# First feed-forward: the 512 columns of the gate and up products streamed in other orders

## The chip, the cores and the metric

The kernel runs on one core of a Trainium2 chip. The metric is the time in device microseconds of one execution. Two runs of the kernel before took 3107.92 and 3108.51 us, median 3108.22.

## The reference

Two transformer blocks for 256 tokens of width 2048, all in float32. The part that the change touches is the first feed-forward of the first block, with 5632 inner columns:

```python
def _swiglu(h, w_gu, w_down):
    gate, up = jnp.split(h @ w_gu, 2, axis=-1)
    return (jax.nn.silu(gate) * up) @ w_down

x = x + ... _swiglu(_rmsnorm(x, ffn1_norm), ffn1_w_gu, ffn1_w_down)   # first feed-forward
# then token mixing, a second feed-forward of the same size, and a second block of two layers
```

`h @ w_gu` is a product of 256 x 2048 by 2048 x 11264. It is summed over the 2048 rows of `w_gu`, column by column, so no column of the result depends on any other column.

## The kernel before

**Slabs.** All large weights come from memory as a stream of slabs of 512 KB. In the feed-forwards a slab is two chunks of 128 rows by 512 columns, so in each of the 128 partitions it holds 2 x 512 floats, one chunk behind the other. SyncE (SP) issues the DMA of a slab into `stage`, a ring of four. ScalarE rounds it into the high part (L1411, semaphore `hi_done`), and GpSimd (L777, `lo_pool`) or VectorE (L1830, `lo_vec`), by turns, subtracts to get the low part. Both parts lie in `split_slabs`, again a ring of four. Its type is float32r. The activations are split likewise into `h_split` (`hx` in the code).

**Products of a slab.** `wide_passes` (L889 to L905) forms the three products high x high, low activations x high weights, and high activations x low weights. Here the activations are the stationary operand and the weights are the moving one: a matmul takes 128 x 128 activations and streams 512 columns of the slab against them, and the result is 128 tokens by 512 columns, which is one whole PSUM bank. A slab has eight matmuls on its high part (L898: two chunks, two halves of the tokens, two parts of the activations), which wait for `hi_done`, and then four on its low part (L903), which wait for the subtraction. All twelve stream 512 neighbouring columns.

**Sums.** `ffn` (L966 on) goes through eleven groups `j` of 512 inner columns. For each it sums eight slabs for the gate (`side` 0) and eight for the up product (`side` 1), `q` = 0 to 7, into one pair of banks, one bank for each half of the tokens. The first matmul of a sum (`q` = 0) starts the bank anew; all others add to what is there. Behind slab `q` = 2 of the gate side stand eight transposes of the group before (`turn_act`, L816), and at some slabs two small matmuls for another part of the program (`ada_reduce`, L957). VectorE and ScalarE read the finished banks column by column in the ordinary order.

**Order.** Each engine runs its instructions in the order in which the program lists them; the semaphores above tie the engines together. A slab's place in `split_slabs` comes free when TensorE's last matmul on it is done (`slab_done`), and its place in `stage` when the low part has been formed.

After the eleven groups, the down product (44 columns of 128 activations, 88 slabs) runs through the same `wide_passes`, then token mixing with slabs of four chunks by 256 columns (`split_passes`, L817 to L835), in which the weights are stationary and 256 columns of activations are streamed (L826, L832). In between stand small matmuls for other parts of the program; those of L1052 are on plain float32 data.

Of the kernel before, what the change touches and what calls it, by code (L numbers as in the profile page):

```python
# [25 lines left out]
P = 128  # L26
# [13 lines left out]
WN, WK = 512, 2  # L40
# [26 lines left out]
def bank_pairs():  # L67


    pairs = []  # L70
    for first, groups, ups in ((G_F1, FFN_GROUPS, GU_GROUPS), (G_MIX, MIX_GROUPS, 0), (G_F2, FFN_GROUPS, GU_GROUPS),
                               (G_LAY[0], LAY_GROUPS, 0), (G_LAY[1], LAY_GROUPS, 0)):
        start = 1 - pairs[-1] if pairs else 0
        pairs += [1 - start] * ups + [(start + i) % 2 for i in range(groups - ups)]
    return pairs


PAIR = bank_pairs()
# [10 lines left out]
def proj_at(p):  # L89

    return S_MIX + 4 * p + 2 * min(max(p - CMP_P0, 0), CMP_STEPS)


S_CG = proj_at(PROJ)
S_GATES = S_CG + 4

# [164 lines left out]
def build(nc, a, out, const, marks, final):  # L261

    ctx = ExitStack()
    with ctx:
# [3 lines left out]
        def sbr(name, shape):  # L268
            return ctx.enter_context(nc.sbuf_tensor(name, shape, F32R))
# [9 lines left out]
        hx = sbr("h_split", [P, 2, DC, S])  # L279
# [40 lines left out]
        ps = ctx.enter_context(nc.psum_tensor("ps", [P, 8, 512], F32))  # L320
# [198 lines left out]
        def slab_split(n):  # L519

            return (lo_vec, nth_vec[n]) if n in by_vector else (lo_pool, nth_pool[n])
# [5 lines left out]
        def slab_part(n, which, width=SLAB):  # L527

            return (ws if in_wide_ring(n) else narrow_ws)[:, slot[n], which, 0:width]
# [13 lines left out]
        def gate_acc(f):  # L543

            return 1 - PAIR[(G_F1, G_F2)[f]]
# [265 lines left out]
        def _(pe):  # L811
            mm = nc.tensor.matmul

            def transpose(dst, src):
                n = src.shape[0]
                return nc.tensor.transpose(dst, src, ident[0:n, 0:n])  # L816
# [71 lines left out]
                    low(2)  # L888
                    low(3)  # L889

            def wide_passes(pair, n, stationary, first, last):

                w = [slab_part(n, i).rearrange("p (c w) -> p c w", c=WK) for i in range(2)]
                pe.wait_ge(hi_done, nth[n])
                for kk in range(WK):
                    for T in range(TT):
                        for i in range(2):
                            mm(ps[:, 2 * pair + T, :], stationary(kk, i)[:, T * P:(T + 1) * P], w[0][:, kk, :],  # L898
                               start=first and kk == 0 and i == 0, stop=False)
                pe.wait_ge(*slab_split(n))  # L900
                for kk in range(WK):
                    for T in range(TT):
                        ins = mm(ps[:, 2 * pair + T, :], stationary(kk, 0)[:, T * P:(T + 1) * P], w[1][:, kk, :],  # L903
                                 start=False, stop=last and kk == WK - 1)
                ins.then_inc(slab_done, 1)  # L905

# [43 lines left out]
            def ada_reduce(f, b):  # L950
                if f + b == 0:
                    pe.wait_ge(*act_out.after("ones"))
                pe.wait_ge(ada_split_done, ADA_GROUPS * f + b + 1)
                if ADA_GROUPS * f + b > 0:
                    pe.wait_ge(ada_picked, ADA_GROUPS * f + b)
                for i in range(2):
                    last = mm(ps[:, 4, :], ones_r[:, :], ada_split[:, i, :], start=i == 0, stop=i == 1)  # L957
                last.then_inc(ada_red, 1)

            def turn_act(f, j):  # L960

                at = GU_GROUPS * f + j
                pe.wait_ge(evacuated, (G_F1, G_F2)[f] + j + 1)
                if at == 0:
                    pe.wait_ge(*vec_out.after("par", len(PARAM_TILES) - 1))
                if at > 0:  # L966
                    pe.wait_ge(act_lo, at)
                for c in range(4):
                    for T in range(TT):
                        last = transpose(ps[:, 6 + c // 2, (c % 2) * S + T * P:(c % 2) * S + (T + 1) * P],  # L970
                                         u(SILU, P, TT, WN)[:, T, c * P:(c + 1) * P])
                last.then_inc(act_turned, 1)

            def ffn(f, s0, g0, r):
                def between(i):
                    for b in range(ADA_GROUPS):
                        if ADA_AT[8 * b + 7] + ADA_SUM == i:
                            ada_reduce(f, b)

                for j in range(GU_GROUPS):  # L980
                    for side in range(2):
                        if side == 0 and j > 0:
                            pe.wait_ge(silu_done, GU_GROUPS * f + j)
                        elif g0 + j > 0:
                            pe.wait_ge(evacuated, g0 + j if side else g0 - 1)
                        for q in range(8):
                            n = s0 + 16 * j + 8 * side + q
                            if j == 0 and side == 0 and q % 2 == 0:
                                pe.wait_ge(*h_ready.after(r, q // 2))
                            wide_passes(PAIR[g0] if side else gate_acc(f), n, lambda kk, i, q=q: hx[:, i, WK * q + kk, :], q == 0, q == 7)  # L990
                            if side == 0 and q == 2 and j > 0:
                                turn_act(f, j - 1)
                            if (f, j, side) == (0, 0, 0) and q in (0, 1):
                                turn_first(2 + q)
                            if (f, j, side, q) == (0, 0, 1, 5):
                                turn_late_params()
                            if (f, j, side, q) == (1, 0, 0, 1):
                                turn_x(2, 3)
                            between(n - s0)
                s1, g1 = s0 + GU_SLABS, g0 + GU_GROUPS  # L1000
                for d in range(DOWN_GROUPS):
                    if d == 0:
                        pe.wait_ge(silu_done, GU_GROUPS * (f + 1))
                        pe.wait_ge(act_lo, GU_GROUPS * (f + 1) - 1)
                    else:
                        pe.wait_ge(evacuated, g1 + d - 1)
                    for q in range(DOWN):
                        n = s1 + DOWN * d + q
                        if d == 0 and q == DOWN - 2:
                            pe.wait_ge(act_lo, GU_GROUPS * (f + 1))  # L1010
                        act_ = lambda kk, i, q=q: ats[:, i, (WK * q + kk) * S:(WK * q + kk + 1) * S]
                        if (d, q) == (DOWN_GROUPS - 1, DOWN - 1):
                            last_passes(PAIR[g1 + d], n, act_, r + 1)
                        else:
                            wide_passes(PAIR[g1 + d], n, act_, q == 0, q == DOWN - 1)
                        if d == 0 and q == 2:
                            turn_act(f, GU_GROUPS - 1)
                        if f == 0 and d > 0 and q == 6:
                            turn_x(1, d - 1)
                        between(n - s0)  # L1020
# [13 lines left out]
            def turn_first(b):  # L1034
                pe.wait_ge(x_in[b], 32)
                turn_x(0, b)
# [76 lines left out]
            gg, sA = G_MIX + PROJ, S_GATES  # L1113
            product(gg, S_CG, outs=1)
            proj_lag(PROJ - 1)
# [79 lines left out]
            first = units_mix()  # L1195
# [11 lines left out]
            for step in range(len(first)):  # L1207
# [9 lines left out]
                if step == 0:  # L1217
                    pe.wait_ge(evacuated, gg + 1)
                    pe.wait_ge(*act_out.after("vn", PROJ - 1))
                    for T in range(TT):  # L1220
                        last = transpose(ps[:, 7, T * 36:T * 36 + 36], u(CTMP, 36, S)[:, T * P:(T + 1) * P])
# [8 lines left out]
            g, n = gg + 1 + GATES, sA + 4 * GATES  # L1230
            pe.wait_ge(*heads_ready.after(0))
            for _k in range(4):
                for half in range(2):
                    pe.wait_ge(evacuated, g - 1)
                    last = split_passes(acc(g), n, heads(0), True, True, chunks=2, width=512, col0=half * W2)
# [39 lines left out]
            for l in range(2):  # L1275
                s0, g0 = S_LAY[l], G_LAY[l]
# [15 lines left out]
                for p in range(PIECE):  # L1292
# [20 lines left out]
                    if 19 <= p < 23:  # L1313
# [5 lines left out]
                        for i, (part, tab) in enumerate(((0, "dcos"), (1, "dsin"))):  # L1319
                            for T in range(TT):  # L1320
                                last = mm(ps[:, 7, i * S:i * S + HALF], fp[:, T, part, :], cst(tab)[:, T * HALF:(T + 1) * HALF],
                                          start=i == 0 and T == 0, stop=i == 1 and T == 1)
                        last.then_inc(*pe_out.mark("fy", l, c))
                    if 18 <= p < 22:
# [7 lines left out]
                        for T in range(TT):  # L1332
                            last = mm(ps[:, 6, T * S:(T + 1) * S], fx[:, c, T * P:(T + 1) * P], cst("dft"), start=True, stop=True)
# [11 lines left out]
                g, n = g0 + PIECE, s0 + 4 * PIECE  # L1345
# [21 lines left out]
                g, n = g + 4, n + 4  # L1367
# [378 lines left out]
        def _(dve):  # L1746
# [231 lines left out]
            for p in range(PROJ + 1):  # L1978
# [29 lines left out]
                if p == CMP_GROUP + 1:  # L2008
# [15 lines left out]
                    last.then_inc(*vec_out.mark("cblk"))  # L2024
            sg, gg, sA = S_CG, G_MIX + PROJ, S_GATES
            dve.wait_ge(slab_done, sA)
# [460 lines left out]
```

## Time and profile before

| what | value |
|---|---|
| median of two runs | 3108.22 us |
| span of the profiled execution, first to last instruction | 3105.2 us |
| TensorE busy in it | 3070.2 us (99%) |
| VectorE, ScalarE, GpSimd busy | 1952.8, 1447.7, 1270.0 us |
| DMA, mean rate | 213 GB/s |
| mean granted TensorE clock | 0.997 of full speed |

The profile is of one execution, whose own time is known only as its span; the median of the runs is 3.0 us longer. The page lists busy time by engine, but TensorE's matmuls overlap each other, so that the mean duration of one (392 ns for 512 columns) is the time from its start to its end and not the time that it adds. What a matmul adds is read from the chain of waits, where consecutive matmuls stand with the time that they take together.

### The profile page before, as it was taken

Reading aid. Unit: us, or ns where it says so; the run is one execution under the profiler, and the core shown is the slowest. Engines: PE = TensorE matmul, PEld = TensorE weight load, DVE = VectorE, ACT = ScalarE, POOL = GpSimd, SP = SyncE. Lnnn points to the kernel's source line nnn. Section 1 sums busy time; section 2 is a strip of 40 time slices with the busy share of each in tenths; the row PEclk is TensorE's granted clock in tenths of the full one; section 3 lists DMA queues with packets and bytes.
Section 4 is the critical chain, followed back from the end, with each engine's and each line's share of the span. In section 5 each row is a group of like instructions: output and inputs, shape, how many; then the busy total and the mean of one; then the engine's idle time right before and its main releaser. Section 6 shows DMA issues by size and latency. Waiting matters only on the chain.

```text
span 3105.2 us, 46479 instructions
## 1 busy us (share of the span) xinstructions
PE 3070.2 (99%) x19038; PEld 2713.0 (87%) x19038; DVE 1952.8 (63%) x2398; ACT 1447.7 (47%) x1877; POOL 1270.0 (41%) x621
## 2 busy tenths in 40 slices
PE   8999999999999999999999999999999999999998
PEld 7888888888999999998888888888899998899986
DVE  5778576673323446773467667677469864589764
ACT  6444444444567545544544444344444454544444
POOL 4444444444566554584444444444610004510013
PEclk9999999999999999999999999999999999999999
DMA  7878777785776565565787778787666545565454
GB/s 230 284 245 282 260 268 268 252 283 175 218 177 181 156 168 145 150 172 195 237 270 257 273 252 276 244 290 246 191 181 190 158 142 199 166 191 178 155 166 166
DMA packets 486653, 662.74 MB, mean 213 GB/s; under 512 B 67992, under 2 KB 273544, under 8 KB 486184
## 3 DMA queue, kind: packets, MB, share of 16 engines
q1 hardware_dynamic: 480952, 655.05, 66.1%
q0 software_dynamic: 4448, 2.94, 0.4%
q8 instruction: 150, 2.46, 0.3%
q10 hardware_dynamic: 1040, 1.78, 0.2%
q14 instruction: 63, 0.52, 0.1%
HBM read 655.47 MB, written 2.10 MB: 212 GB/s over the span
## 4 chain that ended last, share of the span: by engine, by line
PE 97%; DVE 1%; ACT 1%; issue 0%; DMA 0%; POOL 0%; ACTq 0%; DVEq 0%
PE ps L898 36%; PE ps L826 23%; PE ps L903 18%; PE ps L832 11%; PE ps L816 2%; PE ps L857 1%; PE ps L1356 1%; PE ps L1144 1%; PE ps L1125 1%; PE ps L957 0%; PE ps L1052 0%; PE ps L1152 0%; PE ps L1182 0%; PE ps L1174 0%; PE ps L1191 0%
## 5 line engine op out<-in xcount | busy, mean ns | idle before, releaser
L777 POOL TENSOR_TENSOR split_slabs<-stage,split_slabs 128x1024 fp32r<-128x1024 f32 x296 | 749.8, 2534 | 1365.6 <-ACT split_slabs L1411 1365.6
L1411 ACT ACTIVATE split_slabs<-stage 128x1024 fp32r<-128x1024 f32 x592 | 627.6, 1062 | 903.7 <-PE ps L903 665.1
L898 PE MATMUL ps<-split_slabs,h_split 128*128 128x512 f32 x3312 | 827.1, 392 | 0.9 <-ACT split_slabs L1411 0.9
L1411 ACT ACTIVATE narrow_split_slabs<-stage 128x1024 fp32r<-128x1024 f32 (+1 forms) x440 | 461.0, 1052 | 651.2 <-PE ps L832 568.1
L826 PE MATMUL ps<-h_split,narrow_split_slabs 128*128 128x256 f32 x5856 | 748.4, 280 | 0.0
L898 PEld LDWEIGHTS ps<-split_slabs,h_split 128*128 128x128 f32 x3312 | 620.8, 188 | 133.8 <-issue 5.1
L826 PEld LDWEIGHTS ps<-h_split,narrow_split_slabs 128*128 128x128 f32 x5856 | 702.8, 188 | 15.7 <-issue 12.0
L1830 DVE TENSOR_TENSOR split_slabs<-stage,split_slabs 128x1024 fp32r<-128x1024 f32 x296 | 412.2, 1395 | 368.2 <-ACT split_slabs L1411 368.1
L777 POOL TENSOR_TENSOR narrow_split_slabs<-stage,narrow_split_slabs 128x1024 fp32r<-128x1024 f32 (+1 forms) x181 | 436.0, 2418 | 315.0 <-ACT narrow_split_slabs L1411 307.3
L1830 DVE TENSOR_TENSOR narrow_split_slabs<-stage,narrow_split_slabs 128x1024 fp32r<-128x1024 f32 x259 | 333.1, 1288 | 175.8 <-ACT narrow_split_slabs L1411 174.9
L903 PE MATMUL ps<-split_slabs,h_split 128*128 128x512 f32 x1656 | 443.0, 389 | 0.3 <-POOL split_slabs L777 0.3
L832 PE MATMUL ps<-h_split,narrow_split_slabs 128*128 128x256 f32 x2928 | 397.8, 278 | 1.6 <-POOL narrow_split_slabs L777 1.4
L903 PEld LDWEIGHTS ps<-split_slabs,h_split 128*128 128x128 f32 x1656 | 310.9, 188 | 65.9 <-POOL split_slabs L777 0.7
L832 PEld LDWEIGHTS ps<-h_split,narrow_split_slabs 128*128 128x128 f32 x2928 | 364.2, 188 | 2.6 <-POOL narrow_split_slabs L777 2.0
L898 PE MATMUL ps<-split_slabs,act_split 128*128 128x512 f32 x1392 | 344.6, 390 | 0.0
L898 PEld LDWEIGHTS ps<-split_slabs,act_split 128*128 128x128 f32 x1392 | 260.9, 188 | 54.2
L1843 DVE SCALAR_TENSOR_TENSOR U<-U,cact 128x512 f32<-128x512 f32 x168 | 213.6, 1271 | 5.1 <-DMA U<-in_w_ada 4.7
L1846 DVE SCALAR_TENSOR_TENSOR U<-U,cact 128x512 f32<-128x512 f32 x192 | 201.3, 1048 | 6.8
L903 PE MATMUL ps<-split_slabs,act_split 128*128 128x512 f32 x696 | 186.1, 389 | 0.0
L903 PEld LDWEIGHTS ps<-split_slabs,act_split 128*128 128x128 f32 x696 | 130.6, 188 | 27.4
L1857 DVE TENSOR_TENSOR ps<-ps,base_consts 128x512 f32<-128x512 f32 x24 | 16.8, 700 | 162.1 <-PE ps L957 162.1
L2191 DVE SCALAR_TENSOR_TENSOR U<-U,params 128x256 f32<-128x256 f32 x240 | 110.8, 503 | 0.0
(250 smaller groups left out, 2129.4 us busy)
## 6 DMA issues: line engine op xcount, KB each, us to landing
stage<-in_w_in SPq DMA_DIRECT2D x360, 512.0 KB, 3.7
stage<-in_ffn_w_gu SPq DMA_DIRECT2D x352, 512.0 KB, 4.8
U<-in_w_ada SPq DMA_DIRECT2D x192, 512.0 KB, 5.6
stage<-in_ffn_w_down SPq DMA_DIRECT2D x176, 512.0 KB, 5.6
stage<-in_w_out SPq DMA_DIRECT2D x96, 512.0 KB, 4.1
stage<-in_w_in SPq DMA_DIRECT2D x80, 128.0 KB, 2.9
stage<-in_w_branch_c SPq DMA_DIRECT2D x32, 192.0 KB, 3.3
stage<-in_cmp_w SPq DMA_DIRECT2D x8, 512.0 KB, 5.8
```

Of the source, the lines that this page charges most:

```text
L777: nc.gpsimd.tensor_tensor(slab_part(n, 1, size(n)), stage[:, n % RING, 0:size(n)], slab_part(n, 0, size(n)).bitcast(F32), ALU.subtract).th ...
L816: return nc.tensor.transpose(dst, src, ident[0:n, 0:n])
L826: mm(bank[:, c * S:(c + 1) * S], w[0][:, kk, at:at + P], moving(kk, i), start=first and c == 0 and kk == 0 and i == 0, stop=False)
L832: ins = mm(bank[:, c * S:(c + 1) * S], w[1][:, kk, at:at + P], moving(kk, 0), start=False, stop=last and c == outs - 1 and kk == chunks - 1)
L857: ins = mm(acc(g)[:, c * S:(c + 1) * S], w[:, kk, c * P:(c + 1) * P], hx[:, i, KC * k + kk, :], start=first and c == 0 and kk == 0, stop=l ...
L898: mm(ps[:, 2 * pair + T, :], stationary(kk, i)[:, T * P:(T + 1) * P], w[0][:, kk, :], start=first and kk == 0 and i == 0, stop=False)
L903: ins = mm(ps[:, 2 * pair + T, :], stationary(kk, 0)[:, T * P:(T + 1) * P], w[1][:, kk, :], start=False, stop=last and kk == WK - 1)
L1411: return fn(slab_part(n, 0, size(n)), stage[:, n % RING, 0:size(n)], ACT.Copy)
L1830: v.tensor_tensor(slab_part(n, 1), stage[:, n % RING, :], slab_part(n, 0).bitcast(F32), ALU.subtract).then_inc(lo_vec, 1)
L1843: ins = v.scalar_tensor_tensor(total, w[:, 0, :], cact[:, 2 * k:2 * k + 1], total, ALU.mult, ALU.add)
L1846: v.scalar_tensor_tensor(total, w[:, 1, :], cact[:, 2 * k + 1:2 * k + 2], total, ALU.mult, ALU.add).then_inc(ada_load, 1)
L2191: ins = v.scalar_tensor_tensor(cy[:, c, :], src, col, cy[:, c, :], ALU.mult, ALU.add)
```

## The change

`wide_passes` gets two more arguments, `parts` and `run`. With `parts` above 1 it passes the same 512 columns of the slab, and the same 512 columns of the PSUM bank, in another order: the 512 columns are cut into `parts` neighbouring parts of equal width, and the matmul streams `run` columns of the first part, `run` of the second and so on, then the next `run` of each. Both operands get the same order, so each column's result lands where it did, and the order in which each element's sum is formed does not change.

A table gives the order of each slab of a sum by `q`. It is used in the first feed-forward only, and from the third group on (`j` > 1). The entry of `q` = 0 is the ordinary order.

| q | parts | run (columns) | runs in a matmul | shape of the stream |
|---|---|---|---|---|
| 0 | 1 | 512 | 1 | 512 |
| 1 | 2 | 4 | 128 | 64 x 2 x 4 |
| 2 | 2 | 16 | 32 | 16 x 2 x 16 |
| 3 | 2 | 2 | 256 | 128 x 2 x 2 |
| 4 | 4 | 4 | 128 | 32 x 4 x 4 |
| 5 | 2 | 32 | 16 | 8 x 2 x 32 |
| 6 | 2 | 64 | 8 | 4 x 2 x 64 |
| 7 | 8 | 4 | 128 | 16 x 8 x 4 |

```diff
+STREAMS = ((1, WN), (2, 4), (2, 16), (2, 2), (4, 4), (2, 32), (2, 64), (8, 4))
...
-            def wide_passes(pair, n, stationary, first, last):
+            def wide_passes(pair, n, stationary, first, last, parts=1, run=WN):
+
+                def order(cols):
+                    if parts == 1:
+                        return cols
+                    return cols.rearrange("p (h j i) -> p j h i", h=parts, i=run)
...
-                            mm(ps[:, 2 * pair + T, :], stationary(kk, i)[:, T * P:(T + 1) * P], w[0][:, kk, :],
+                            mm(order(ps[:, 2 * pair + T, :]), stationary(kk, i)[:, T * P:(T + 1) * P], order(w[0][:, kk, :]),
...
-                        ins = mm(ps[:, 2 * pair + T, :], stationary(kk, 0)[:, T * P:(T + 1) * P], w[1][:, kk, :],
+                        ins = mm(order(ps[:, 2 * pair + T, :]), stationary(kk, 0)[:, T * P:(T + 1) * P], order(w[1][:, kk, :]),
...
-                            wide_passes(PAIR[g0] if side else gate_acc(f), n, lambda kk, i, q=q: hx[:, i, WK * q + kk, :], q == 0, q == 7)
+                            wide_passes(PAIR[g0] if side else gate_acc(f), n, lambda kk, i, q=q: hx[:, i, WK * q + kk, :], q == 0, q == 7,
+                                        *(STREAMS[q] if f == 0 and j > 1 else ()))
```

On TensorE, at the start of the third group's gate slabs (`q` = 0, 1, 2 and the transposes behind them), the order before is:

```order
L903 MATMUL ps<-split_slabs,h_split 128x512 [waits lo_pool]
L903 MATMUL ps<-split_slabs,h_split 128x512 x3
L898 MATMUL ps<-split_slabs,h_split 128x512 [waits hi_done]
L898 MATMUL ps<-split_slabs,h_split 128x512 x7
L903 MATMUL ps<-split_slabs,h_split 128x512 [waits lo_vec]
L903 MATMUL ps<-split_slabs,h_split 128x512 x3
L898 MATMUL ps<-split_slabs,h_split 128x512 [waits hi_done]
L898 MATMUL ps<-split_slabs,h_split 128x512 x7
L903 MATMUL ps<-split_slabs,h_split 128x512 [waits lo_pool]
L903 MATMUL ps<-split_slabs,h_split 128x512 x3
L816 MATMUL ps<-base_consts,U 128x128 [waits act_lo,evacuated]
```

and at the same place after the change, where L904 and L909 are the former L898 and L903, and the shape lists the stream's loops from the outermost:

```order
L909 MATMUL ps<-split_slabs,h_split 128x512 [waits lo_pool]
L909 MATMUL ps<-split_slabs,h_split 128x512 x3
L904 MATMUL ps<-split_slabs,h_split 128x64x2x4 [waits hi_done]
L904 MATMUL ps<-split_slabs,h_split 128x64x2x4 x7
L909 MATMUL ps<-split_slabs,h_split 128x64x2x4 [waits lo_vec]
L909 MATMUL ps<-split_slabs,h_split 128x64x2x4 x3
L904 MATMUL ps<-split_slabs,h_split 128x16x2x16 [waits hi_done]
L904 MATMUL ps<-split_slabs,h_split 128x16x2x16 x7
L909 MATMUL ps<-split_slabs,h_split 128x16x2x16 [waits lo_pool]
L909 MATMUL ps<-split_slabs,h_split 128x16x2x16 x3
L817 MATMUL ps<-base_consts,U 128x128 [waits act_lo,evacuated]
```

Nothing has moved: each row stands where it stood, with the same waits and the same number of matmuls, and only the shapes of `q` = 1 and `q` = 2 differ.

On TensorE at the end of the last group, where the down product (`act_split`) begins, after the change:

```order
L904 MATMUL ps<-split_slabs,h_split 128x4x2x64 [waits hi_done]
L904 MATMUL ps<-split_slabs,h_split 128x4x2x64 x7
L909 MATMUL ps<-split_slabs,h_split 128x4x2x64 [waits lo_pool]
L909 MATMUL ps<-split_slabs,h_split 128x4x2x64 x3
L904 MATMUL ps<-split_slabs,h_split 128x16x8x4 [waits hi_done]
L904 MATMUL ps<-split_slabs,h_split 128x16x8x4 x7
L909 MATMUL ps<-split_slabs,h_split 128x16x8x4 [waits lo_vec]
L909 MATMUL ps<-split_slabs,h_split 128x16x8x4 x3
L904 MATMUL ps<-split_slabs,act_split 128x512 [waits hi_done,act_lo,silu_done]
```

The last slab of the sum has eight parts; the down product behind it streams 512 neighbouring columns as before.

## Rows read from the trace of the kernel before

**Rows 1.** The page: busy microseconds, share of the span, instructions.

```profile
PE 3070.2 (99%) x19038; PEld 2713.0 (87%) x19038; DVE 1952.8 (63%) x2398; ACT 1447.7 (47%) x1877; POOL 1270.0 (41%) x621
```

**Rows 2.** Chain that ended last, start of the third group: start us, us, what.

```profile
105.83 0.23 PE ps L903
106.06 1.81 PE ps L898 x8
107.87 0.91 PE ps L903 x4
108.78 1.81 PE ps L898 x8
...
114.22 0.87 PE ps L816 x8
```

**Rows 3.** The same chain inside the fifth group, and at the down product's start.

```profile
207.71 1.81 PE ps L898 x8
209.52 0.91 PE ps L903 x4
...
224.03 1.81 PE ps L898 x8
...
226.75 0.46 PE ps L957 x2
227.21 1.85 PE ps L898 x8
...
510.31 1.81 PE ps L898 x8
```

**Rows 4.** Windows: busy us of each engine, granted clock, DMA share, GB/s.

```profile
106.00:510.30 404.30, 404.17 (x1818) 334.75 (x1817) 292.30 (x280) 171.75 (x180) 184.60 (x73) 1.00 0.79 265
510.30:570.00 59.70, 59.70 (x269) 49.47 (x268) 35.52 (x35) 22.70 (x23) 24.33 (x11) 1.00 0.76 253
```

**Rows 5.** Waits that ended between 106.0 and 510.3 us: total, times, longest.

```profile
POOL split_slabs L777 <- ACT split_slabs L1411: 222.7, 73, 5.2
ACT split_slabs L1411 <- PE ps L903: 165.4, 105, 2.2
ACT split_slabs L1411 <- DMA stage<-in_ffn_w_gu: 64.0, 34, 4.2
```

**Rows 6.** Groups of instructions between 106.0 and 510.3 us: busy, mean ns, idle before.

```profile
L777 POOL TENSOR_TENSOR split_slabs<-stage,split_slabs 128x1024 fp32r<-128x1024 f32 x73 | 187.0, 2562 | 222.7 <-ACT split_slabs L1411 222.7
L1411 ACT ACTIVATE split_slabs<-stage 128x1024 fp32r<-128x1024 f32 x144 | 153.0, 1062 | 232.5 <-PE ps L903 165.4 <-DMA stage<-in_ffn_w_gu 64.0 <-DMA stage<-in_ffn_w_down 3.1
```

**Rows 7.** The chain in token mixing, with matmuls of 256 columns.

```profile
850.95 1.81 PE ps L826 x16
852.77 0.91 PE ps L832 x8
853.67 1.81 PE ps L826 x16
855.49 0.91 PE ps L832 x8
856.39 1.81 PE ps L826 x16
...
859.12 0.86 PE ps L1052 x2
859.97 1.88 PE ps L826 x16
861.86 0.94 PE ps L832 x8
```

## The prediction

> **What bounds the kernel.** I read the busy times first: TensorE is busy for 99% of the span, and no other engine for more than 63% [rows 1]. That alone decides little, because a TensorE that is busy may be a slow one, so I went on to the chain of work that ended last, in the stretch of the change. The third group of the first feed-forward begins at 106.06 us [rows 2]; the down product begins at 510.31 us [rows 3]. Between them the chain is TensorE's matmuls, one after the other: eight on the high part in 1.81 us, four on the low part in 0.91 us, the next slab at once. The reader should see that the starts leave no gap: from 207.71 to 224.03 us lie six slabs, 2.72 us each [rows 3], so a matmul adds 2.72 / 12 = 0.2267 us, and a column 0.443 ns.
>
> The windows say the same for the whole stretch: TensorE busy 404.17 of 404.30 us at a granted clock of 1.00, that is 2.4 GHz, the DMA engines at 0.79 [rows 4]. The waits that end there are all of the suppliers: GpSimd waits for ScalarE, and ScalarE waits for TensorE to give slab places back (105 times, 165.4 us) more than for weights to land (34 times, 64.0 us) [rows 5]. The suppliers are ahead, the matmuls set the pace, and what a matmul gains or loses is gained or lost by the program.
>
> **What changes.** From group 3 to 11 there are 9 x 16 = 144 slabs. Those with `q` = 0 keep their order, one in eight; 126 slabs, 126 x 12 = 1512 matmuls, get another. They take 1512 x 0.2267 = 342.7 us now. (As a check of the stretch: 144 slabs x 2.72 = 391.7, nine times eight transposes at 0.87 = 7.8 [rows 2], eight pairs of the small matmuls at 0.46 = 3.7 [rows 3], together 403.2 of the 404.25 us; the rest are the matmuls just behind such small ones, 1.84 or 1.85 for eight.)
>
> *Instructions.* None is added, removed or moved; the waits are the same, DMAs and all other engines' work too. The price of that is 0, with nothing that has to hide it. Readers of the banks find each column where it was. The start of a sum, which has to prepare the whole bank, keeps the ordinary order.
>
> *The one unknown: what it costs to leave neighbouring columns.* The seven orders cut a matmul into 128, 32, 256, 128, 16, 8 and 128 runs, 696 in all. Each order is used by 9 x 2 x 12 = 216 matmuls, so 696 x 216 = 150,300 runs take the place of 1512. At each, TensorE must read the slab and write the bank somewhere else. No matmul of the program before streams its columns in such a way, so I bound it from both sides.
>
> Downwards: 512 columns at one per cycle of 2.4 GHz would be 213.3 ns, and a matmul adds 226.7. If the new order could remove all of the 13.3 ns, which nothing in the trace suggests, that is 1512 x 13.3 ns = 20 us less. More cannot come from these matmuls unless a column takes less than a cycle.
>
> Upwards, the nearest row is the start of a matmul, which also moves to another address in both memories. In token mixing a matmul streams 256 columns, and sixteen take 1.81 us, just as eight of 512 do; two slabs, from 850.95 to 856.39 us, take 5.44 us with 48 matmuls [rows 7], as two wide ones do with 24. So 24 more moves cost less than the 0.01 us that the rows resolve: at most 0.4 ns each, and 0 as measured. On 150,300 runs the end of that bound is 150,300 x 0.4 ns = 60 us. **I take 0**, since this is the only row in which the number of moves doubles and the time shows nothing; what speaks for caution is that the hardware may hide a move between two matmuls and not one inside.
>
> A second thing that the rows show: the time per column is not quite fixed. After two matmuls of L1052 the same sixteen take 1.88 us instead of 1.81 [rows 7], for several slabs. If the new orders brought that on for all 1512, it would be 1512 x 0.2267 x 0.07 / 1.81 = 13 us.
>
> **Sum.** The profiled execution stays at 3105.2 + 0 us; with the 3.0 us by which the median of the runs lies above its span, 3108.2. The stretch has no one who could turn a loss into less: after it the down product is again TensorE alone, busy 59.70 of 59.70 us [rows 4], so a loss passes on whole. A gain would pass too: for a slab in 2.56 us instead of 2.72, ScalarE needs 1.06, GpSimd 2.56 for every second slab [rows 6], and the DMA share would go from 0.79 to 0.84.
>
> The Trainium skill, page "Advanced Engine Details and Errata", section "Memory Cachelines", has two sentences that point apart here. One says that a matmul is slowed significantly by any pattern in PSUM that is not contiguous; by it all 1512 matmuls pay. The other says that every two consecutive elements should be contiguous for best throughput, with PSUM lines of two fp32 values; by it none pays, since the shortest run here is two columns that begin at an even one. It gives SBUF lines of 16 bytes and asks for two hits on a line, which a run of two also has. No row of this trace can decide between them.
>
> **The rivals.** A measurement of this kernel can tell about 2%, 62 us, from no change. On 1512 matmuls that is 41 ns each, 18% more than 226.7.
>
> *A. No cost, 3108 us: 0.67.* For it are the rows on the start of matmuls, and that runs of two columns or more never ask for a single one. A small drift of the time per column (3121 with the 13 us, 3088 with the 20 us gain) belongs here too; to the gain I give 0.02 of these. A lowering that merges the pattern back into 512 neighbouring columns would look the same in time, though the shapes above speak against it.
>
> *B. Only the finest order pays: 0.08.* If runs of two are too short for the reading or the writing side and a matmul of `q` = 3 takes twice its time, that is 216 x 0.2267 = 49 us: 3157. Still within 2%.
>
> *C. Each run costs a pause: 0.17. This is the one on the other side.* The place is the column stream of TensorE at the end of each run. If a pause is one column's time, 0.443 ns, it is 150,300 x 0.443 ns = 67 us, 3175 us (+2.1%); if it is two, 133 us, 3241 us. It decides from 62 us / 150,300 = 0.41 ns per run, just beyond what rows 7 leave open. For it: the 13.3 ns above the bare cycles grow with the columns, not with the number of matmuls [rows 7], so something in the stream itself does pause now and then, and it may be a change of address.
>
> *D. Any order but the ordinary one runs at half rate: 0.08.* Then the 1512 matmuls cost 342.7 us more: 3451 us. It is what the skill's first sentence would give if "significantly" were a factor of two. Against it: the pair of columns, the smallest piece that a change of rate would rest on, is never broken here.
>
> **The numbers.** The forecast is A, 3108 us, slightly more likely than all the rest. The range goes from 3098 (noise and a part of the gain) to 3180, which takes in B and the cheaper half of C: about 0.82. Within 2% are A and B, 0.75; slower by more are C and D, 0.25 less what of C falls under 62 us, so 0.24; faster by more than 2% has no mechanism, since the whole gain ends at 20 us, and gets 0.01.
>
> **What the profile after would show.** In the groups of instructions with shapes kept apart, the 1512 matmuls appear with their loops; mean durations should stay at 389 to 392 ns for all. The chain should show 1.81 and 0.91 us for each slab whatever its `q`, and the down product should begin at 510.3 us. Under C the pieces differ by order: `q` = 3 the longest (256 runs; 0.11 us more per matmul at one column's time), `q` = 1, 4 and 7 half as much, `q` = 5 and 6 nearly nothing. Under B only `q` = 3 differs; under D all seven alike, 3.6 us for eight. In each of these ScalarE's waits for TensorE grow and its waits for landing weights go. The forecast is wrong if one order's eight matmuls take more than 1.9 us, and I would be wrong about the bound if TensorE lost time in the stretch while they all took 1.81.

## The result and the profile after

The changed kernel takes 3159.36 us (two runs, 3158.71 and 3160.02), against 3108.22 before: ratio 1.0168, 95% interval 1.0152 to 1.0184, 51 us slower. The span of its profiled execution is 3158.2 us, 53.0 longer than before.

The page's first line, to be read against [rows 1]:

```profile
PE 3122.9 (99%) x19038; PEld 2717.6 (86%) x19038; DVE 1930.6 (61%) x2398; ACT 1450.1 (46%) x1877; POOL 1266.4 (40%) x621
```

The same instructions, and 52.7 us more of busy TensorE; the weight loads (PEld), at 2717.6 us, are only 4.6 us longer. The windows from the start of the third group to the down product, and behind it (columns as in [rows 4]):

```profile
106.62:564.50 457.88, 457.88 (x1817) 340.09 (x1817) 270.34 (x281) 174.16 (x180) 181.74 (x73) 1.00 0.71 235
564.50:624.20 59.70, 59.70 (x268) 49.44 (x267) 33.14 (x35) 23.28 (x23) 24.65 (x11) 1.00 0.74 250
```

Where the third group and the down product begin, the chain has

```profile
106.62 1.81 PE ps L904 x8
...
564.46 1.86 PE ps L904 x8
```

The stretch of the change has grown from 404.25 to 457.8 us at an unchanged granted clock and with TensorE busy throughout, while its DMA share has fallen from 0.79 to 0.71. All of the loss lies there. The waits in it, against [rows 5]:

```profile
POOL split_slabs L778 <- ACT split_slabs L1418: 279.2, 73, 6.3
ACT split_slabs L1418 <- PE ps L909: 249.0, 128, 3.5
...
ACT split_slabs L1418 <- DMA stage<-in_ffn_w_gu: 34.1, 15, 4.2
```

ScalarE waits longer for TensorE and less for weights: the suppliers were slowed by TensorE, not TensorE by them. What TensorE does with the time stands in the chain (start us, us, what; the high parts of one sum, `q` = 1 to 7, then `q` = 0 of the next):

```profile
135.41 2.01 PE ps L904 x8
...
138.42 1.92 PE ps L904 x8
...
141.30 2.63 PE ps L904 x8
...
145.24 2.14 PE ps L904 x8
...
148.45 1.89 PE ps L904 x8
...
151.29 1.83 PE ps L904 x8
...
154.03 2.23 PE ps L904 x8
...
157.37 1.86 PE ps L904 x8
...
160.14 1.01 PE ps L904 x4
```

From one start to the next is the time of a whole slab, twelve matmuls; less the 2.72 us of before and divided by 12, it gives each order its price:

| q | parts, run | slab, us | more per matmul, ns |
|---|---|---|---|
| 1 | 2, 4 | 3.01 | 24 |
| 2 | 2, 16 | 2.88 | 13 |
| 3 | 2, 2 | 3.94 | 102 |
| 4 | 4, 4 | 3.21 | 41 |
| 5 | 2, 32 | 2.84 | 10 |
| 6 | 2, 64 | 2.74 | 2 |
| 7 | 8, 4 | 3.34 | 52 |
| 0 | ordinary, behind q = 7 | 2.77 | 4 |

A sum of eight slabs takes 24.73 us instead of 21.76. Times 18 sums that is 53.5 us, the whole growth of the stretch.

### The profile page after: what moved, and what is told of

Read it like the earlier page. It is cut to its first block, busy times and chain, and to the rows that moved or that the text cites. A ratio compares the mean times of both kernels' runs of the same rounds, so it can differ in the third digit from the quotient of the medians.

```text
span 3158.2 us, 46479 instructions
## 1 busy us (share of the span) xinstructions
PE 3122.9 (99%) x19038; PEld 2717.6 (86%) x19038; DVE 1930.6 (61%) x2398; ACT 1450.1 (46%) x1877; POOL 1266.4 (40%) x621
## 4 chain that ended last, share of the span: by engine, by line
PE 97%; DVE 1%; ACT 1%; issue 0%; DMA 0%; POOL 0%; ACTq 0%; DVEq 0%
PE ps L904 36%; PE ps L827 23%; PE ps L909 18%; PE ps L833 11%; PE ps L817 2%; PE ps L858 1%; PE ps L1363 1%; PE ps L1151 1%; PE ps L1132 1%; PE ps L963 0%; PE ps L1059 0%; PE ps L1189 0%; PE ps L1159 0%; PE ps L1181 0%; DMA x_res<-in_x 0%
## 5 line engine op out<-in xcount | busy, mean ns | idle before, releaser
L904 PE MATMUL ps<-split_slabs,h_split 128*128 128x512 f32 x3312 | 863.9, 404 | 0.9 <-ACT split_slabs L1418 0.9
L904 PEld LDWEIGHTS ps<-split_slabs,h_split 128*128 128x128 f32 x3312 | 624.4, 189 | 165.3 <-issue 6.5
L1837 DVE TENSOR_TENSOR split_slabs<-stage,split_slabs 128x1024 fp32r<-128x1024 f32 x296 | 402.9, 1364 | 423.2 <-ACT split_slabs L1418 423.1
L909 PE MATMUL ps<-split_slabs,h_split 128*128 128x512 f32 x1656 | 461.4, 401 | 0.3 <-POOL split_slabs L778 0.3
L909 PEld LDWEIGHTS ps<-split_slabs,h_split 128*128 128x128 f32 x1656 | 312.8, 189 | 82.0 <-POOL split_slabs L778 0.7
L904 PE MATMUL ps<-split_slabs,act_split 128*128 128x512 f32 x1392 | 344.7, 390 | 0.0
L904 PEld LDWEIGHTS ps<-split_slabs,act_split 128*128 128x128 f32 x1392 | 260.9, 188 | 54.4
L1853 DVE SCALAR_TENSOR_TENSOR U<-U,cact 128x512 f32<-128x512 f32 x192 | 201.4, 1049 | 6.8
L1850 DVE SCALAR_TENSOR_TENSOR U<-U,cact 128x512 f32<-128x512 f32 x168 | 196.7, 1171 | 9.2 <-DMA U<-in_w_ada 8.5
L909 PE MATMUL ps<-split_slabs,act_split 128*128 128x512 f32 x696 | 186.1, 389 | 0.0
L909 PEld LDWEIGHTS ps<-split_slabs,act_split 128*128 128x128 f32 x696 | 130.6, 188 | 27.4
```

Of the source, the lines that this page charges most:

```text
L904: mm(order(ps[:, 2 * pair + T, :]), stationary(kk, i)[:, T * P:(T + 1) * P], order(w[0][:, kk, :]), start=first and kk == 0 and i == 0, st ...
L909: ins = mm(order(ps[:, 2 * pair + T, :]), stationary(kk, 0)[:, T * P:(T + 1) * P], order(w[1][:, kk, :]), start=False, stop=last and kk == ...
L1837: v.tensor_tensor(slab_part(n, 1), stage[:, n % RING, :], slab_part(n, 0).bitcast(F32), ALU.subtract).then_inc(lo_vec, 1)
L1850: ins = v.scalar_tensor_tensor(total, w[:, 0, :], cact[:, 2 * k:2 * k + 1], total, ALU.mult, ALU.add)
L1853: v.scalar_tensor_tensor(total, w[:, 1, :], cact[:, 2 * k + 1:2 * k + 2], total, ALU.mult, ALU.add).then_inc(ada_load, 1)
```

## The experiments

Each kernel but the last has eight places in its table, so one run gives up to seven prices. They are read as above: from the start of one slab's matmuls to the next in the chain, well inside the stretch. All edits are against the changed kernel.

**Reading or writing?** First the reads in the new orders and the writes in the ordinary one (here the matmul on the high part, cut; the one on the low part is changed alike, here and below):

```diff
-mm(order(ps[:, 2 * pair + T, :]), stationary(kk, i)[...], order(w[0][:, kk, :]),
+mm(ps[:, 2 * pair + T, :], stationary(kk, i)[...], order(w[0][:, kk, :]),
```

> The weights are read from the slab in the orders of the change, and the results are written to neighbouring columns of the bank, so columns land in wrong places. In the chain of the changed kernel a matmul of q = 1 to 7 adds 24, 13, 101, 41, 10, 2 and 51 ns to the 226.7 of the ordinary order; times 216 that is 52 us. Theory R (the price is paid where the slab is read): the same seven additions and 3159 us. Theory W (it is paid where the bank is written): 2.72 us for every slab and 3108 us. Theory B of the prediction, that only the order of two-column runs pays, is already refuted by the seven additions. If both sides have a price of their own, this run and the next each show a part, and the parts say whether they add or the larger one rules.

Measured: 3161.11 us, ratio to before 1.0169 (1.014 to 1.0199), and the same seven durations as in the changed kernel to 0.01 us; at `q` = 3 and 7:

```profile
140.07 2.63 PE ps L904 x8
...
152.79 2.23 PE ps L904 x8
```

Then the mirror of it:

```diff
-mm(order(ps[:, 2 * pair + T, :]), stationary(kk, i)[...], order(w[0][:, kk, :]),
+mm(order(ps[:, 2 * pair + T, :]), stationary(kk, i)[...], w[0][:, kk, :],
```

> The mirror of the run before: the slab is read in neighbouring columns, and the results are written to the bank in the orders of the change. Theory W: the seven additions of 24, 13, 101, 41, 10, 2 and 51 ns and 3159 us. Theory R: 3108 us and 2.72 us for each slab. The Trainium skill, page Advanced Engine Details and Errata, section Memory Cachelines, names the bank's side as the one that slows matmuls in any order that is not contiguous; that is theory W.

Measured: 3110.68 us, ratio 1.0006 (0.9995 to 1.0018). Its chain, here at two slabs whose writes have different orders:

```profile
136.95 1.81 PE ps L904 x8
138.76 0.91 PE ps L909 x4
139.67 1.81 PE ps L904 x8
141.49 0.91 PE ps L909 x4
```

The whole price is on the side where the slab is read. To leave neighbouring columns in the bank, in runs of two or more, costs nothing, although the Trainium skill says that any pattern that is not contiguous slows matmuls ("Advanced Engine Details and Errata", section "Memory Cachelines").

**The length of a run**, with two parts throughout:

```diff
+STREAMS = ((1, WN), (2, 2), (2, 4), (2, 8), (2, 16), (2, 32), (2, 64), (2, 128))
```

> All orders have two parts; the run is 2, 4, 8, 16, 32, 64, 128 columns for q = 1 to 7; reads and writes alike, so the result is complete. One fixed pause per run (0.4 ns, as runs of 2 and of 16 show in the changed kernel) would give additions of 101, 51, 26, 13, 7, 3, 2 ns, together 203 ns, 44 us, 3152 us; but the change measured 24 for runs of 4, against that. A price that depends on how a run lies in some line of the memory gives 101, 24, about 18, 13, 10, 2, 1: 169 ns, 36 us, 3145 us. What decides is whether 8 lies under 16 plus a factor of two, and whether the price falls with the number of runs at all between 4 and 32.

Measured: 3149.64 us, ratio 1.0132 (1.0103 to 1.0162). The slabs take 4.08, 3.00, 2.92, 2.88, 2.84, 2.76 and 2.72 us: additions of 113, 23, 17, 13, 10, 3 and 0 ns. A fixed pause per run falls: from 2 to 4 columns the number of runs halves and the price falls to a fifth, from 4 to 16 the number falls to a quarter and the price only by half. The runs of two take one and a half times the ordinary 2.72 us:

```profile
157.90 2.71 PE ps L904 x8
160.62 1.36 PE ps L909 x4
```

(The 3.94 us of the changed kernel for the same order, behind another neighbour, is a little less; right behind the eight transposes, at 166.90 us, it takes 4.08 us there too.)

**The distance between runs**, at runs of four:

```diff
+STREAMS = ((1, WN), (2, 4), (4, 4), (8, 4), (16, 4), (32, 4), (64, 4), (2, 8))
```

> Runs of four columns throughout, in 2, 4, 8, 16, 32 and 64 parts for q = 1 to 6 (the move from one run to the next is then 256, 128, 64, 32, 16 and 8 columns), and two parts with runs of eight for q = 7. Theory 'distance' (a move is the dearer the farther it goes, and free within a short row of memory): the changed kernel shows the reverse for 256, 128 and 64 columns (24, 41, 51 ns), so additions would have to turn and fall to near 0 at 16 and 8 columns. Theory 'loops' (the price belongs to stepping the outer loops, or to returning to an earlier part): additions of 24, 41, 51 and then about 55 for all others, sum about 300 ns, 65 us, 3173 us. Theory 'same place in the banked memory' (moves that are multiples of a large power of two columns differ from small ones): 16 and 8 columns differ from 256 in a way that follows neither.

Measured: 3137.79 us, ratio 1.0094 (1.0065 to 1.0123). The first six orders have 128 runs each. In the chain of this kernel the orders of 4, 8, 16, 32, 64 parts and then (2,8) follow:

```profile
137.30 2.14 PE ps L904 x8
...
140.52 2.23 PE ps L904 x8
...
143.87 1.96 PE ps L904 x8
...
146.82 1.80 PE ps L904 x8
...
149.52 1.85 PE ps L904 x8
...
152.30 1.95 PE ps L904 x8
```

So the slabs take 3.22, 3.35, 2.95, 2.70, 2.78 us. The order (32,4), with 128 runs that lie 16 columns apart, is no dearer than neighbouring columns, even 0.02 us cheaper. This refutes 'loops' and with it every theory in which leaving a run costs something by itself; where the next run lies decides, and not by a simple rule: moves by 16 columns cost nothing, by 8 columns 5 ns per matmul, by 32 columns 19 ns, by 64 columns 52 ns and by 256 columns 24 ns.

**Short moves with runs of 2, 8 and 16:**

```diff
+STREAMS = ((1, WN), (32, 8), (32, 2), (64, 2), (128, 2), (16, 16), (16, 8), (8, 16))
```

> Seven orders with many runs and short moves: parts and run are (32,8), (32,2), (64,2), (128,2), (16,16), (16,8), (8,16) for q = 1 to 7, so the distance between one run and the next is 16, 16, 8, 4, 32, 32 and 64 columns. In the run on distances a slab in 32 parts with runs of four took 2.70 us, less than the 2.72 of neighbouring columns, and 64 parts 2.77. Theory 'distance' (what is dear is a move by 64 columns, 256 bytes, or a multiple of it): about 2.70, 2.7, 2.8, 2.8, 2.8, 2.8 us for the first six and 2.9 for (8,16). Theory 'count' (runs of two are dear wherever they go): (32,2), (64,2), (128,2) take 4.1 us like (2,2). A faster order than 2.70 us, down to the 2.56 of one column per cycle, would give a version better than both kernels. Total by 'distance' about 3118 us, by 'count' about 3195.

Measured: 3262.63 us, ratio 1.0492 (1.047 to 1.0514). The slabs take 2.80, 5.19, 5.54, 5.42, 2.87, 2.77 and 2.87 us. Both theories missed for runs of two: they are dear wherever they go, and dearer here (twice the ordinary time) than at 256 columns (one and a half times). The three orders in the chain:

```profile
143.15 3.46 PE ps L904 x8
...
148.34 3.70 PE ps L904 x8
...
153.88 3.61 PE ps L904 x8
```

In (128,2) the stream takes two columns of every four and returns for the others after the whole bank's width; in (2,2) it returns to the same four after two runs. That made me look at groups of four columns, 16 bytes: if each *visit* to such a line costs the time of four columns, 256 visits cost twice 128, unless the second visit comes while the line is still at hand.

**The distance alone.** The reads take pairs of runs, the second `away` columns behind the first, so that loops and number of runs are the same for all:

```diff
-                    return cols.rearrange("p (h j i) -> p j h i", h=parts, i=run)
+                    one = cols[:, 0:1]
+                    return bass.AP(one.tensor, one.offset, [one.ap[0], [run, WN // (2 * run)], [away, 2], [1, run]])
```

Runs of four, with `away` = 252, 240, 224, 192, 128, 64, 16:

> Reads alone, writes to neighbouring columns. Always 64 pairs of runs of four columns; the second run of a pair lies 252, 240, 224, 192, 128, 64, 16 columns behind the first (q = 1 to 7), so number and length of runs and the loops are the same for all, and only the distance differs. Some columns are read twice and others not, so the sums are of other columns. Known: at 256 columns 3.01 us for a slab. Theory 'multiples of 64 columns': 192, 128 and 64 cost about 3.0 us as 256 does; 252, 240 and 16 about 2.7 to 2.75; 224 (32 beyond a multiple) between. Theory 'far moves': 252 to 128 all about 3.0, falling only at 64 and 16.

Measured: one run, 3140.53 us; slabs of 2.92, 2.92, 2.88, 3.01, 3.00, 3.00 and 2.88 us. The three multiples of 64 columns agree with the 3.01 of 256, and 'far moves' falls, since 224 and 240 are cheaper than 64. But the others cost 0.16 to 0.20 us, where near nothing was expected, so multiples of 64 are only part of it: of the 24 ns that a matmul pays at 256 columns, 13 to 17 are paid at 252, 240, 224 and 16 columns too. The orders of 224 and 192 in the chain:

```profile
138.45 1.92 PE ps L905 x8
...
141.33 2.01 PE ps L905 x8
```

Runs of two, `away` = 256, 254, 240, 224, 192, 64, 16:

> The same with runs of two columns: 128 pairs, the second run 256, 254, 240, 224, 192, 64, 16 columns behind the first (q = 1 to 7); reads alone. Known: at 256, with writes in the same order, 3.94 to 4.08 us for a slab. Theory 'multiples of 64 columns': 256, 192, 64 near 4.0, the others well under it. Theory 'half a line' (a run of two wastes half of each 16-byte line, the rule of two hits for a line in the Trainium skill, page Advanced Engine Details and Errata, section Memory Cachelines, would still call it free): all seven near 4.0, or, by the skill's rule, all near 2.72 but for what the distance adds.

Measured: one run, 3265.16 us; slabs of 4.07, 3.96, 3.93, 3.92, 3.99, 4.00 and 3.92 us. All near 4.0: 'half a line' holds, and the distance hardly matters beside it. In all seven, the first runs of the pairs visit each group of four columns twice, the second time two runs later, and so do the second runs. The last order moves by 16 columns as (32,2) does, which took 5.19 us instead of 3.92; there the second visit comes 32 runs later.

**The line as the unit.** Only the alignment differs between the orders of each pair (0 or 2 columns into a group of four):

```diff
+STREAMS = ((1,), (2, (0, 32, 8, 16, 16, 4)), (2, (2, 32, 8, 16, 16, 4)), (2, (0, 64, 4, 16, 16, 8)), (2, (2, 64, 4, 16, 16, 8)), (2, (0, 0, 1, 56, 8, 64)), (2, (2, 0, 1, 56, 8, 64)), (2, (0, 16, 8, 12, 32, 2)))
-                    return cols.rearrange("p (h j i) -> p j h i", h=parts, i=run)
+                    at, s1, n1, s2, n2, run = shape
+                    one = cols[:, at:at + 1]
+                    return bass.AP(one.tensor, one.offset, [one.ap[0], *([[s1, n1]] if n1 > 1 else []), [s2, n2], [1, run]])
```

> Reads alone, each order 512 columns, some read twice, so the sums are of other columns. Theory 'line' (the reader fetches 16-byte lines of four columns, and each visit to a line costs as much as four neighbouring columns, 1.77 ns, however few of the four are used; a line used again soon is cheaper): the price follows the visits to lines, 128 in the ordinary order. q = 1, runs of four, aligned, 16 columns apart (128 visits): about 2.7 to 2.9 us for a slab. q = 2, the same begun two columns later, so that each run lies across two lines (256 visits): about 5.4. q = 3, runs of eight, aligned (128): about 2.8. q = 4, the same two columns later (192): about 4.1. q = 5, runs of 64, aligned (128): about 2.75. q = 6, two columns later (136): about 2.9. q = 7, runs of two in separate lines (256): 5.4, as the three such orders of the run on short distances (5.2 to 5.5). Theory 'length of run' (a run of four is long enough wherever it begins): q = 2, 4 and 6 as q = 1, 3 and 5.

Measured: one run, 3235.61 us. The chain, `q` = 1 to 7 and the next 0 (L906 is the line of the high part):

```profile
138.78 1.85 PE ps L906 x8
...
141.56 3.56 PE ps L906 x8
...
146.92 1.87 PE ps L906 x8
...
149.72 2.64 PE ps L906 x8
...
153.69 1.86 PE ps L906 x8
...
156.49 1.90 PE ps L906 x8
...
159.35 3.62 PE ps L906 x8
...
164.75 1.85 PE ps L906 x8
```

| run, columns into the line | visits to lines | expected slab, us | measured |
|---|---|---|---|
| 4, 0 | 128 | 2.7 to 2.9 | 2.78 |
| 4, 2 | 256 | 5.4 | 5.36 |
| 8, 0 | 128 | 2.8 | 2.80 |
| 8, 2 | 192 | 4.1 | 3.97 |
| 64, 0 | 128 | 2.75 | 2.80 |
| 64, 2 | 136 | 2.9 | 2.86 |
| 2, 0 | 256 | 5.4 | 5.40 |

A run of four doubles the slab's time when it begins two columns later, with everything else the same. The reader pays by visits to 16-byte lines: 226.7 ns for 128 visits, 1.77 ns each. (All slabs here have elements of 4 bytes; whether the unit is 16 bytes or four elements, no run shows.) For `q` = 3, with 256 visits, the rule alone gives 5.44 us where 3.94 were measured. That the second visit is cheaper because it comes two runs later is the reading of the runs on distance; no run varies that delay alone.

**The writing side at its worst**, with reads in the ordinary order:

```diff
+STREAMS = ((1, WN), (32, 4), (32, 2), (64, 2), (128, 2), (2, 2), (8, 4), (2, 64))
```

> Reads in the ordinary order, writes to the bank in the orders (32,4), (32,2), (64,2), (128,2), (2,2), (8,4), (2,64), so runs of two whose distance is 4 to 256 columns; results land in wrong columns. Reading in the second to fourth of these took 5.2 to 5.5 us for a slab. If the bank takes pairs of columns anywhere at full rate, every slab stays at 2.72 us and the time at 3108; if its lines are as the slab's, the three cost 5.4 and the time is about 3250.

Measured: 3110.31 us, ratio 1.0003 (0.9993 to 1.0013), and 1.81 and 0.91 us at every slab. The bank takes pairs of columns in any of these orders at full rate.

**Moves by 64 columns.** The edit is that of the two runs on distance, but with `[[run, WN // (parts * run)], [away, parts], [1, run]]`, parts = 8 and `away` = 64, 60, 56, 48, 40, 32, 20:

> Reads alone, runs of four columns, always 16 x 8 runs; the eight runs of a set lie 64, 60, 56, 48, 40, 32, 20 columns apart (q = 1 to 7), so 112 of the 127 moves have that distance and every order visits 128 lines. Some columns are read twice, so the sums are of other columns. At 64 columns the change took 3.34 us for a slab (with writes in the same order). Theory 'multiples of 64 columns' (256 bytes; fitted to 24, 42 and 52 ns at 64, 96 and 112 such moves, 0.46 ns each): 3.34 us at 64 and 2.7 to 2.8 at 60, 56, 48, 40 and 20, with 32 between, about 2.9. Theory 'far moves': the price falls smoothly with the distance, so 60 and 56 lie near 3.3.

Measured: one run, 3131.89 us. The chain, `q` = 1 to 7 and the next 0 (L905 is the line of the high part):

```profile
133.51 2.23 PE ps L905 x8
...
136.85 1.90 PE ps L905 x8
...
139.70 1.88 PE ps L905 x8
...
142.52 1.84 PE ps L905 x8
...
145.29 1.94 PE ps L905 x8
...
148.19 1.87 PE ps L905 x8
...
150.98 1.82 PE ps L905 x8
...
153.71 1.83 PE ps L905 x8
```

The slabs take 3.34, 2.85, 2.82, 2.77, 2.90, 2.79 and 2.73 us. From 64 to 60 columns four fifths of the price go, although the move is nearly as far. A move by 64 columns, 256 bytes, is dear: 52 ns over 112 such moves, 0.46 ns each, or 0.37 ns if the 11 ns that 60 columns pay are taken off. The rest, 1 to 15 ns per matmul with no order in the distance that I can name, stays open; moves by 32 columns pay 6 ns here and paid 19 in (16,4).

**The dearest order undone:**

```diff
-STREAMS = ((1, WN), (2, 4), (2, 16), (2, 2), (4, 4), (2, 32), (2, 64), (8, 4))
+STREAMS = ((1, WN), (2, 4), (2, 16), (1, WN), (4, 4), (2, 32), (2, 64), (8, 4))
```

> The change with the ordinary order for q = 3; its runs of two are undone and all else stays. If the prices per order add up and pass whole to the end, 216 matmuls give back 101 ns each: 22 us, 3137 us. If TensorE's loss at q = 3 was partly a wait that moves elsewhere, less comes back.

Measured: 3143.15 us, ratio to before 1.0108 (1.0092 to 1.0125): 16 us less than the change, where 22 were expected. The down product's matmuls (minimum, median and maximum ns; first and last start), of the changed kernel and of this one:

```profile
L904 PE MATMUL ps<-split_slabs,act_split x1392: 387/389/477, 564.3 to 2264.3; 128*128 128x512 f32 x199
```

```profile
L904 PE MATMUL ps<-split_slabs,act_split x1392: 387/389/477, 541.0 to 2242.6; 128*128 128x512 f32 x199
```

At the end of the stretch it is 23.3 us ahead, 1.0 of it from before the third group, so the stretch gives back 22.3 us, as the prices say. The 6 us that are missing were lost behind it, where the two kernels are alike. In the profiled executions 4 of them lie between the last matmul of L920 on `act_split` and the first on `h_split`: 434.5 us in the changed kernel (2267.4 to 2701.9), 438.3 in this one (2245.8 to 2684.1), 438.5 in the kernel before and 435.8 to 439.8 in the other runs. There the changed kernel's profiled execution was quick, rather than this one slow. What made it so is open; the kernel before ranged from 3106.14 to 3114.51 us on the same chip in the same comparison.

**The order (32,4) for all 619 wide slabs:**

```diff
-            def wide_passes(pair, n, stationary, first, last, parts=1, run=WN):
+            def wide_passes(pair, n, stationary, first, last, parts=32, run=4):
```

(with the argument for the table left out of the call)

> The one order that was faster than the ordinary one, 32 parts with runs of four (2.70 us for a slab against 2.72), for every wide slab of the program: 619 slabs. If the 0.02 us hold for all, 12 us less: 3096 us, ratio 0.996. If the gain came only from its place between slower orders, no difference, 3108.

Measured: 3096.40 us over five runs, ratio to before 0.996 (0.9947 to 0.9974). It beats both kernels, the one before (3107.92 us in the same comparison) by 11.5 us: small, but clear of the noise. In its chain the gain is not even:

```profile
219.99 1.79 PE ps L903 x8
221.78 0.89 PE ps L908 x4
...
225.36 0.46 PE ps L962 x2
225.82 1.81 PE ps L903 x8
```

Some stretches run at 2.68 us for a slab (219.99 to 222.67), others at 2.72 like the ordinary order. The mean matches the forecast. Between 93 and 746 us every change from one rate to the other stands right behind small matmuls, mostly the two of L962: to 2.72 behind those at 225.36 us, back to 2.68 behind those at 278.34. Not all small matmuls bring a change, and what in them does it is open.

## Why the prediction was wrong

**The bound held.** TensorE's matmuls set the pace, nothing hid them, and the loss passed whole to the end: 53.6 us in the stretch, 53.0 in the span. The suppliers' waits moved as foretold.

**The step that failed is the one unknown, where I took 0 for each of the 150,300 runs.** The row on which I took it, sixteen matmuls of 256 columns in the time of eight of 512, compared the *number* of moves. The experiments show that the number is not what is paid: 128 runs cost nothing at 16 columns apart and 52 ns at 64. What is paid is (a) visits to 16-byte lines of the slab, and (b) the distance from one line to the next, most at multiples of 256 bytes. A matmul of that row streams 256 neighbouring columns from a multiple of 256, so, if the tile itself begins at a line's start, two such matmuls make no visit more than one of 512, and that row could not have shown (a). I had said that the hardware might hide a move between two matmuls and not one inside; the upper end that I kept from the same row, 60 us, took in the 53 us, but as a bound on moves it was right by its size only: the 16 runs of (2,32) pay 10 ns, 0.6 ns each and not at most 0.4. That the range takes in the measured time is luck. And the forecast of 0, called "slightly more likely than all the rest" there, had 0.67 against 0.33, twice as much as all the rest; that was too sure for one row.

**Rival B** gave 3157 us, 2 from the measured time, and is wrong all the same. It had only `q` = 3 pay, a whole matmul's time each; `q` = 3 pays 102 ns, 22 of the 53 us, and undoing it left 3143 us. The seven prices in one chain refute what the total alone would have confirmed.

**Rival C**, a pause for each run, came near in shape (0.11 us foretold for `q` = 3, 0.102 measured; half as much for runs of four, 24 to 52 ns measured), with 67 us against 53. Its mechanism fell with the orders of 32 and 64 parts.

**Rival D** fell in the changed kernel itself, where (2,64) pays 2 ns. The sentence of the Trainium skill on it ("Advanced Engine Details and Errata", section "Memory Cachelines") is refuted for these runs by the two kernels that only write in the new orders, ratio 1.0006 and 1.0003. The other sentence on PSUM there, by which two consecutive elements should be contiguous, agrees with both; no run writes single columns. For SBUF, where the slab lies, the same section asks for at least two hits on a 16-byte line. Two did not keep the rate here: two columns per visit took up to twice the time of four.

**By terms**, the 53.5 us are: `q` = 3, whose 256 visits to 128 lines make it, 216 x 102 ns = 22 us; the three orders with runs of four, 216 x 117 ns = 25 us, which 0.46 ns for each move by a multiple of 64 columns fits (64, 96 and 112 such moves are 29, 44 and 52 ns, against 24, 41 and 52); the three with long runs, 216 x 25 ns = 5.4 us; and 1 us at the ordinary slab behind `q` = 7. The 0.46 ns are a fit and no mechanism. With eight parts 11 of the 52 ns stay at 60 columns, and with two parts 13 to 17 of the 24 ns stay at distances that are no multiple. For long runs they do not always do: (2,16) has 16 moves by 256 columns, 7 ns, and pays 13, while (8,16) has 28 moves by 64 columns, 13 ns, and pays 12 or 13. That part is open.

## What to carry to other kernels

Count the 16-byte lines that a float32r moving operand visits, not the runs: keep runs whole lines long and aligned to them. The order in which lines come then cost 0 to 19 ns of a matmul's 227 here, and up to 52 ns where successive lines lie a multiple of 256 bytes apart. The order of the output columns in PSUM, in runs of two or more, cost nothing in any form tried. And when several variants share one kernel, read them apart in the chain before a total is laid to one of them.

## What the hardware showed unasked

- An order with a jump behind every run can be faster than neighbouring columns: (32,4) in 2.68 to 2.72 us for a slab, ratio 0.996 over the program, and which of the two rates it gets changes only behind small matmuls.
- Runs of two, which visit every line twice, take half as much again when the second visit comes two runs later (4.08 us against 2.72), and twice the time when it comes much later (5.42).
- A slab in the ordinary order takes up to 2.77 us right behind one in another order (`q` = 0 behind `q` = 7): the reader carries something over from matmul to matmul. It is the reader, since the kernel that only reads in the new orders shows the same 2.77 us and the one that only writes in them 2.72.
